# A two-layer transformer kernel on one core: the modulation weights in column quarters, each followed by a quarter of the first projection

## The chip, the cores and the metric

One core of a Trainium2 chip runs the whole program. The metric is the device time of one execution in microseconds (us), as the median of several. TensorE multiplies into eight accumulation banks; ScalarE (ACT), VectorE (DVE) and GpSimd (POOL) prepare operands and read results; SyncE (SP) only issues DMA transfers. The engines run side by side and meet at semaphores.

## The reference

The program is a hybrid attention layer followed by a second layer with a recurrent mixer, latent attention and a large feed-forward part. All data are float32, one batch of 256 tokens, width 2048. The change touches the start of the first layer only:

```
mod = silu(c) @ w_ada + b_ada                      # c: 2048, w_ada: 2048 x 6144
shift, scale, gate = split(mod, 3)
h = rms_norm(x, g_norm) * (1 + scale) + shift      # x: 256 x 2048
proj = h @ w_in                                    # 2048 x 9296
qa, ka, va, za, q_idx, k_idx, w_idx, qb, kb, vb, zb = split(proj)
k_idx = rms_norm(k_idx)
score = sum over 16 index heads of w_idx * relu(q_idx . k_idx)   # per query and key
# the 64 best keys of each query (top_k of score) are kept in attention a
```

`h` at feature f needs `scale` and `shift` at f alone, but a sum over f in `h @ w_in` needs every feature of `h` in the end. The third part of `mod`, the gate, is used after attention and stays where it was.

## The kernel before

**Operands.** A float32 product is made of three single-pass products: each operand is split into a high and a low part (high times high, high times low, low times high). Activations of 256 tokens lie in `HX`, with the halves `HH` and `HL`, as 16 groups of 128 features. A weight chunk of 512 columns comes in four pieces of 512 rows (1 MB each) through the ring `WR` of `NSLOT` = 4 slots. For each piece ACT writes the high part to `WH` in two halves (the helper `high`, L1400), POOL subtracts to get the low part `WL`, in two halves as well (`low_part`, L541), and PE multiplies (L838 to L840). `WH` holds two pieces, so `high` runs two pieces ahead of PE: it waits for `half_done` and `piece_done`. SP waits for a slot to come free and issues the next load (L577). PE's order is the order of the program's text, piece by piece.

**The start.** `w_ada`'s first 4096 columns are needed for shift and scale. They come as 32 pieces of 1 MB, each 128 rows by 2048 contiguous columns (`ada_row`, L590): 16 for scale, then 16 for shift, through the same ring `WR`. For each, `ada_piece` (L895) makes four matmuls with 32 columns of `CW` (the vector c, 32 times over) into the four partition groups of `BANK[0]` or `BANK[1]`. Between the eighth and the ninth piece PE transposes the parameters (L945) and x (L916). After the sixteenth piece ACT copies the bank to `mod_row`, and `mod_cols` (L903) turns the row into columns; after the thirty-second again. DVE adds the bias (L1788). Then ACT scales and shifts the 16 feature groups of x (L1465), and DVE splits each pair of groups in two instructions (L1799, L1800); `ht_ready` tells PE.

**The index part.** Then come a piece for the index key and the index weights (`n_kw`, 128 columns), and two chunks for the index queries (`n_qi`), with features on partitions (`feat_chunk`, stationary operand the weights, 256 moving columns). The index key is normalised by DVE, turned by PE and copied by ACT to `KB`. Sixteen scoring steps follow (L981): PE multiplies queries with `KB` into `BANK[4]` or `BANK[5]`, ACT takes relu of it (L1491), DVE adds it to the score with two instructions (L1825, L1827). Then DVE alone finds the 64 best keys and builds `bias_a` (L1833 to L1859).

**The branch chunks.** Sixteen chunks follow, eight for branch a (queries 0 and 1, keys 2 and 3, values 4 and 5, gates 6 and 7) and eight for branch b, in a hardware loop over b (`Fori`) on PE, DVE and SP. They have tokens on partitions (`tok_chunk`, 512 moving columns, alternating between the bank pairs 0,1 and 2,3). ACT reads each finished chunk (`read_chunk`, L1413). For the first four of a branch DVE normalises the heads (L1868 to L1875), PE transposes them (L996) into `BANK[4]` to `BANK[7]`, and ACT stores them (L1522). Attention follows, and the rest of the program.

## Time and profile before

| | us |
|---|---|
| median of 3 runs | 2029.04 (2020.97 to 2036.34) |
| profiled execution | 2021.87 |
| its span in the profile | 2020.0 |
| PE busy | 1902.7 (94%) |
| POOL busy | 1327.0 (66%) |
| DVE busy | 911.4 (45%) |
| ACT busy | 810.3 (40%) |

The first two rows are of different executions; the profiled one is 7 us below the median. The span is what the trace covers. "Busy" counts the instructions of an engine that do work; PE's is a sum over overlapping, pipelined matmuls, so that 94% doesn't say that it runs at its best speed.

### The profile page before, as it was taken

To read this page: it belongs to the slowest core of one execution; us is meant where nothing else is said; L and a number is where in the kernel's file an instruction comes from. 1 tells how busy PE (TensorE), PEld (TensorE's weight loads), DVE (VectorE), ACT (ScalarE), POOL (GpSimd) and SP (SyncE) were. 2 spreads that over 40 slices of the span, in tenths; PEclk is the share of its full clock that TensorE was granted. 3 is DMA by queue.
4 is the path that set the end of the run, shared out by engine and by line. 5 is a ranking of instruction groups with operands and counts; after the bars stand their busy time and mean duration, and the time that the engine had idled before them with its cause. 6 is when DMAs were issued, how large, how long until landed. Compare 5 with 4: busy or idle time off the path is not lost.

```text
span 2020.0 us, 32437 instructions
## 1 busy us (share of the span) xinstructions
PE 1902.7 (94%) x13007; PEld 1586.7 (79%) x13007; DVE 911.4 (45%) x1117; ACT 810.3 (40%) x1087; POOL 1327.0 (66%) x671
## 2 busy tenths in 40 slices
PE   5679999999999989998999999899999999999997
PEld 2177788788757779887779978788888888888886
DVE  0035760053063251664754350477655566833323
ACT  2044444444453445333422244444443344443333
POOL 0065888888616858994243279598888888844442
PEclk9689999999999999998999999999999999999999
DMA  8943555555593536553200045455555555555553
GB/s 335 411 154 115 178 187 188 188 185 187 202 344 125 179 114 198 189 190 110 76 24 4 4 150 198 151 189 187 187 188 188 190 189 193 192 190 188 198 196 125
DMA packets 161587, 352.64 MB, mean 175 GB/s; under 512 B 6175, under 2 KB 18861, under 8 KB 154829
## 3 DMA queue, kind: packets, MB, share of 16 engines
q1 hardware_dynamic: 160589, 346.94, 51.1%
q10 hardware_dynamic: 896, 4.20, 0.5%
q8 instruction: 81, 1.33, 0.3%
q14 instruction: 21, 0.17, 0.0%
HBM read 349.02 MB, written 2.10 MB: 174 GB/s over the span
## 4 chain that ended last, share of the span: by engine, by line
PE 59%; POOL 19%; issue 14%; DMA 4%; DVE 2%; ACT 1%; POOLq 0%; DVEq 0%; SPq 0%; ACTq 0%
PE bank L884 20%; POOL WL L541 19%; PE bank L886 10%; PE bank L838 6%; PE bank L840 6%; PE bank L839 6%; PE bank L1185 5%; DMA WR<-in_w_ada 3%; PE bank L1105 1%; PE bank L1115 1%; PE bank L895 1%; PE bank L916 1%; PE bank L1148 0%; DMA WR<-in_w_in 0%; PE bank L917 0%
## 5 line engine op out<-in xcount | busy, mean ns | idle before, releaser
L541 POOL TENSOR_TENSOR WL<-WR,WH 128x1024 fp32r<-128x1024 f32 (+2 forms) x510 | 1232.5, 2429 | 512.5 <-ACT WH L1400 511.3
L1400 ACT ACTIVATE WH<-WR 128x1024 fp32r<-128x1024 f32 (+2 forms) x554 | 576.9, 1047 | 809.6 <-PE bank L840 462.2
L884 PE MATMUL bank<-HX,WH 128*128 128x512 f32 x1840 | 640.3, 392 | 6.5 <-POOL WL L541 5.3
L886 PE MATMUL bank<-HX,WL 128*128 128x256 f32 x1840 | 515.2, 280 | 0.0
L884 PEld LDWEIGHTS bank<-HX,WH 128*128 128x128 f32 x1840 | 344.2, 187 | 83.1 <-issue 6.0
L886 PEld LDWEIGHTS bank<-HX,WL 128*128 128x128 f32 x1840 | 347.7, 189 | 0.0
L838 PE MATMUL bank<-WH,HX 128*128 128x512 f32 (+2 forms) x864 | 335.2, 388 | 12.5 <-POOL WL L541 6.3
L839 PE MATMUL bank<-WL,HX 128*128 128x512 f32 (+2 forms) x864 | 332.5, 385 | 0.0
L840 PE MATMUL bank<-WH,HX 128*128 128x512 f32 (+2 forms) x864 | 332.3, 385 | 0.0
L838 PEld LDWEIGHTS bank<-WH,HX 128*128 128x128 f32 x864 | 163.7, 189 | 45.9 <-issue 11.4
L840 PEld LDWEIGHTS bank<-WH,HX 128*128 128x128 f32 x864 | 163.6, 189 | 30.6
L839 PEld LDWEIGHTS bank<-WL,HX 128*128 128x128 f32 x864 | 163.8, 190 | 30.0 <-issue 0.2
L1951 DVE TENSOR_REDUCE arena<-bank 128x256 f32<-128x512 f32 x115 | 71.3, 681 | 207.7 <-PE bank L886 207.7
L840 PE MATMUL bank<-WH,AL 128*128 128x512 f32 x352 | 137.0, 389 | 0.0
L839 PE MATMUL bank<-WL,AH 128*128 128x512 f32 x352 | 136.9, 389 | 0.0
L838 PE MATMUL bank<-WH,AH 128*128 128x512 f32 x352 | 136.9, 389 | 0.0
L541 DVE TENSOR_TENSOR WL<-WR,WH 128x1024 fp32r<-128x1024 f32 x44 | 53.9, 1226 | 157.9 <-ACT WH L1400 157.8
L895 PE MATMUL bank<-WR,CW 128*32 128x512 f32 x384 | 69.9, 815 | 31.5 <-DMA WR<-in_w_ada 31.5
L2184 DVE SCALAR_TENSOR_TENSOR arena<-arena,cols 128x256 f32<-128x256 f32 x44 | 90.0, 2103 | 1.6 <-DVE arena L2179 1.5
L1875 DVE TENSOR_SCALAR arena<-arena,small 128x128 f32<-128x128 f32 x64 | 61.5, 1030 | 43.1 <-ACT small L1408 43.1
L2189 DVE SCALAR_TENSOR_TENSOR arena<-arena,cols 128x256 f32<-128x256 f32 x44 | 78.8, 1848 | 1.5
L840 PEld LDWEIGHTS bank<-WH,AL 128*128 128x128 f32 x352 | 66.1, 188 | 13.8
(288 smaller groups left out, 1957.6 us busy)
## 6 DMA issues: line engine op xcount, KB each, us to landing
WR<-in_w_in SPq DMA_DIRECT2D x97, 1024.0 KB, 5.0
WR<-in_w_ada SPq DMA_DIRECT2D x48, 1024.0 KB, 7.9
WR<-in_ffn_w_gate SPq DMA_DIRECT2D x44, 1024.0 KB, 5.1
WR<-in_ffn_w_up SPq DMA_DIRECT2D x44, 1024.0 KB, 5.2
WR<-in_ffn_w_down SPq DMA_DIRECT2D x44, 1024.0 KB, 5.0
WR<-in_w_out SPq DMA_DIRECT2D x32, 1024.0 KB, 5.0
WR<-in_w_in SPq DMA_DIRECT2D x12, 768.0 KB, 4.3
WR<-in_mla_w_ukv SPq DMA_DIRECT2D x4, 1024.0 KB, 5.6
```

Source lines behind the costliest of these rows:

```text
L541: eng.tensor_tensor(half(WL, n % NSLOT, *w), half(WR, n % NSLOT, *w), half(WH, nth(n) % 2, *w), ALU.subtract).then_inc(ready, 1)
L838: pe.matmul(out, stat[0], mov[0], start=start, stop=False, skip_group_check=True)
L839: pe.matmul(out, stat[0], mov[1], start=False, stop=False, skip_group_check=True)
L840: return pe.matmul(out, stat[1], mov[0], start=False, stop=stop, skip_group_check=True)
L884: pe.matmul(bank[:, :].rearrange("p (h n) -> p h n", h=2), wh[:, k, o], HX[:, :, kk, :], start=kk == 0, stop=False, skip_group_check=True)
L886: last = pe.matmul(bank[:, 0:L], wl[:, k, o], HX[:, 0, kk, :], start=False, stop=kk == KT - 1, skip_group_check=True)
L895: last = pe.matmul(bank[o, :], CW[:, k, :], WR[:, n % NSLOT, g * CH:(g + 1) * CH], start=k == 0, stop=k == KT - 1)
L1185: last = pe.matmul(o[h, q, :], x(h, q), y(h, q), start=(n == 0), stop=(n == len(terms) - 1))
L1400: act.activation(half(WH, nth(n) % 2, *w), half(WR, n % NSLOT, *w), ACT.Copy).then_inc(hi_ready, 1)
L1951: dve.tensor_reduce(dst, BANK[bank][:, :].rearrange("p (h n) -> p n h", h=2), AX_X, ALU.add).then_inc(ready, 1)
L2184: own.mark(dve.scalar_tensor_tensor(out=CV[:, f, :], in0=RAWF[:, f, 1:L + 1], scalar=w(1), in1=CV[:, f, :], op0=ALU.mult, op1=ALU.add))
L2189: last = dve.scalar_tensor_tensor(out=CV[:, f, :], in0=RAWF[:, f, 0:L], scalar=w(0), in1=CV[:, f, :], op0=ALU.mult, op1=ALU.add)
```

## The change

**Loads.** The 4096 columns of `w_ada` are taken in four column quarters: quarter m holds 512 columns of shift and the same 512 of scale, for all 2048 rows, as 8 pieces of 1 MB (256 rows by 2 times 512 columns), each in two transfers whose contiguous stretch is 512 columns (2 KB). They have a ring of their own in the arena (`ada_w`, four slots of 1 MB, semaphores `ada_in` and `ada_done`). Between them SP loads `w_in`: for each quarter q of the rows, one piece for the index key (128 columns), two for the index queries and one for the first chunk of branch a (`in_piece`).

**Work.** After quarter q of `w_ada`, `mod_cols(q)` gives shift and scale of 4 of the 16 feature groups, which ACT scales and DVE splits. PE then multiplies the rows of quarter q of all four pieces into banks that stay open over the four quarters: `BANK[1]` key, `BANK[4]` to `BANK[7]` queries, `BANK[2]` and `BANK[3]` branch chunk; `BANK[0]` holds the modulation. Between these pieces stand the 8 `mod_piece` of quarter q+1.

**Scores.** The sixteen scoring steps move from before the first branch chunk into chunks 5 and 6 of branch a, one before every second feature group on PE, and one relu before each `high` on ACT. DVE chooses the keys after the fourth chunk of branch a. The loop over b is written out on PE and DVE, and SP's is split in two. The slot numbers of later pieces shift; of the last output projection's loads the third no longer waits for `y_sum`, the fourth does.

The diff, cut to its core:

```diff
-        mod_row = at(4096, 2, CH)
+        mod_row = at(4096, CH)
+        CA = at(4608, KT, 32)
+        ada_w = [at(8192 + PK * CH * i, PK * CH) for i in range(4)]
...
+            w_mod = w_ada[:, 0:2 * D].rearrange("(i k p) (h c n) -> i c p k h n", k=2, p=P, h=2, c=4)
+
+            def ada_quarter(m, first, end):
+
+                for i in range(first, end):
+                    n = 8 * m + i
+                    if n >= 4:
+                        sp.wait_ge(ada_done, n - 3)
+                    for k in range(2):
+                        sp.dma_start(ada_w[n % 4][:, k * 2 * CH:(k + 1) * 2 * CH].rearrange("p (h n) -> p h n", h=2),
+                                     w_mod[i, m, :, k]).then_inc(ada_in[n % 4], 16)
+
+            def in_piece(q, i):
+
+                c0, width = ((KW_COL, P), (IDX_COL, CH), (IDX_COL + CH, CH), (0, CH))[i]
+                src = w_in[q * PK * P:(q + 1) * PK * P, c0:c0 + width]
+                load(n_in + 4 * q + i, src.rearrange("(k p) n -> p k n", p=P), width)
+
+            ada_quarter(0, 0, 4)
...
+            ada_quarter(0, 4, 8)
+            for q in range(4):
+                in_piece(q, 0)
+                in_piece(q, 1)
+                if q < 3:
+                    ada_quarter(q + 1, 0, 3)
+                in_piece(q, 2)
+                if q < 3:
+                    ada_quarter(q + 1, 3, 5)
+                in_piece(q, 3)
+                if q < 3:
+                    ada_quarter(q + 1, 5, 8)
+            with sp.Fori(1, 8) as j:
+                chunk(n_br, w_in, j * CH, CH, shift=j * PIECES)
+            with sp.Fori(0, 8) as j:
+                chunk(n_br + 8 * PIECES, w_in, B_COL + j * CH, CH, shift=j * PIECES)
...
-                elif m == 2:
+                elif m == 3:
...
+            def mod_piece(n):
+
+                i = n % 8
+                pe.wait_ge(ada_in[n % 4], 32 * (n // 4 + 1))
+                if i == 0 and n >= 8:
+                    pe.wait_ge(mod_ready, n // 8)
+                for g in range(4):
+                    o = slice(32 * g, 32 * g + 32)
+                    last = pe.matmul(BANK[0][o, :], CA[:, 2 * i + g // 2, :], ada_w[n % 4][:, g * CH:(g + 1) * CH],
+                                     start=i == 0, stop=i == 7)
+                last.then_inc(ada_done, 1)
+
             def mod_cols(m):
 
                 pe.wait_ge(row_took, m + 1)
                 for j in range(4):
-                    last = pe.matmul(BANK[2 + m][:, 4 * j:4 * j + 4], mod_row[:, m, j * P:(j + 1) * P], group_col,
+                    last = pe.matmul(BANK[0][:, 2 * j:2 * j + 2], mod_row[:, j * P:(j + 1) * P], half_col,
                                      start=True, stop=True)
                 last.then_inc(mod_cols_ready, 1)
...
-            for k in range(KT // 2):
-                ada_piece(n_ada + k, k, BANK[0])
+            for n in range(4):
+                mod_piece(n)
...
-            for k in range(KT // 2, KT):
-                ada_piece(n_ada + k, k, BANK[0])
-            for k in range(KT):
-                ada_piece(n_ada + KT + k, k, BANK[1])
-                if k == 3:
-                    mod_cols(0)
-            mod_cols(1)
...
+            for n in range(4, 8):
+                mod_piece(n)
+            for q in range(4):
+                more = 8 * (q + 1)
+                mod_cols(q)
+                for i, (token, first, width) in enumerate(((False, 1, P), (False, 4, CH), (False, 6, CH), (True, 2, CH))):
+                    if q < 3:
+                        for n in range(*((0, 3), (3, 5), (5, 7), (7, 8))[i]):
+                            mod_piece(more + n)
+                    piece(n_in + 4 * q + i, q, token, first, width)
+                    if q == 3 and i == 1:
+                        pe.wait_ge(kiT_taken, 1)
+                        for t in range(TT):
+                            last = pe.transpose(BANK[0][:, t * P:t * P + P], KIT[:, t * P:(t + 1) * P], ident[:])
+                        last.then_inc(ki_ready, 1)
...
+            def index_from(s):
+
+                def begin(kk):
+                    if kk % 2 == 1:
+                        index_step(s + kk // 2)
+                return begin
+
+            for b in range(2):
                 for j in range(8):
 
+                    if b == 0 and j == 0:
+                        continue
+                    if b == 0 and j == 1:
+                        pe.wait_ge(kb_ready, 1)
                     pe.wait_ge(act_took, b * 16 + 6 + 2 * j - 2)
-                    tok_chunk(n_br + PIECES * j, (j + 1) % 2, CH, more=b * (8 * PIECES))
+                    tok_chunk(n_br + PIECES * j, (j + 1) % 2, CH, more=b * (8 * PIECES),
+                              **(dict(begin=index_from(8 * (j - 5))) if b == 0 and j in (5, 6) else {}))
...
+            for q in range(4):
+                act.wait_ge(ada_done, 8 * (q + 1))
+                act.activation(mod_row, BANK[0][:, :], ACT.Copy).then_inc(row_took, 1)
+                high(n_in + 4 * q)
+                act.wait_ge(mod_ready, q + 1)
+                for k in range(4 * q, 4 * q + 4):
+                    act.activation(xT[:, k, :], xT[:, k, :], ACT.Identity, bias=mod[:, k:k + 1],
+                                   scale=gs[:, k:k + 1]).then_inc(x_scaled, 1)
+                high(n_in + 4 * q + 1)
+                if q == 3:
+                    act.wait_ge(piece_done, n_in + 13)
+                    act.activation(KIT, BANK[1][:, 0:L], ACT.Copy).then_inc(kiT_taken, 1)
+                high(n_in + 4 * q + 2)
+                high(n_in + 4 * q + 3)
...
+                    scoring = b == 0 and j in (5, 6)
+                    relus = lambda p: dict(first=lambda s: index_relu(8 * (j - 5) + 2 * p + s)) if scoring else {}
+                    if b or j:
+                        high(n + 2, more, **relus(0))
+                        high(n + 3, more, **relus(1))
...
+            two_rows = lambda v: v.rearrange("p (h k) -> p h k", h=2)
+            for q in range(4):
+                o = slice(4 * q, 4 * q + 4)
+                dve.wait_ge(mod_cols_ready, q + 1)
+                own.link(dve.tensor_tensor(two_rows(mod[:, 0:2 * KT])[:, :, o],
+                                           BANK[0][:, 0:8].rearrange("p (j h) -> p h j", h=2),
+                                           two_rows(col("b_ada", 0, 2 * KT))[:, :, o], ALU.add))
+                dve.scalar_tensor_tensor(out=gs[:, o], in0=mod[:, KT + 4 * q:KT + 4 * q + 4], scalar=1.0,
+                                         in1=col("g_norm", 4 * q, 4), op0=ALU.add, op1=ALU.mult).then_inc(mod_ready, 1)
+                for g in (2 * q, 2 * q + 1):
+                    k = slice(2 * g, 2 * g + 2)
+                    dve.wait_ge(x_scaled, 2 * (g + 1))
+                    own.link(dve.tensor_copy(HH[:, k, :], xT[:, k, :]))
+                    dve.tensor_tensor(HL[:, k, :], xT[:, k, :], HH[:, k, :], ALU.subtract).then_inc(ht_ready, 1)
...
-            with dve.Fori(0, 2) as b:
-                own.enter(b, 12)
+            for b in range(2):
...
-                own.leave(2)
+                if b == 0:
+                    choose_keys()```

On PE, at the end of the modulation, before: the last two of the 32 pieces, `mod_cols` (L903), and the first products with the index key's weights.

```order
L895 MATMUL bank<-WR,CW 32x512 [waits piece_in2]
L895 MATMUL bank<-WR,CW 32x512 x3
L895 MATMUL bank<-WR,CW 32x512 [waits piece_in3]
L895 MATMUL bank<-WR,CW 32x512 x3
L903 MATMUL bank<-ident,arena 128x4 [waits row_took]
L903 MATMUL bank<-ident,arena 128x4 x3
```

And now, at the end of the first of four quarters: L934 is a modulation piece, L942 `mod_cols`, L865 to L867 the products with the key's piece.

```order
L934 MATMUL bank<-arena 32x512 [waits ada_in3]
L934 MATMUL bank<-arena 32x512 x3
L942 MATMUL bank<-small,arena 128x2 [waits row_took]
L942 MATMUL bank<-small,arena 128x2 x3
L934 MATMUL bank<-arena 32x512 [waits mod_ready,ada_in0]
L934 MATMUL bank<-arena 32x512 x3
L934 MATMUL bank<-arena 32x512 [waits ada_in1]
L934 MATMUL bank<-arena 32x512 x3
L934 MATMUL bank<-arena 32x512 [waits ada_in2]
L934 MATMUL bank<-arena 32x512 x3
L865 MATMUL bank<-HX,WH 128x256 [waits lo_ready,ht_ready]
L866 MATMUL bank<-HX,WH 128x256
```

Products now stand after 8 modulation pieces and `mod_cols`, with three pieces of the next quarter ahead of them; before they stood after all 32.

On SP, the loads after the parameters, before (L590 is `w_ada`, L577 `w_in`):

```order
L590 DMA WR<-in_w_ada 128x2048 [waits piece_done] x28
L577 DMA WR<-in_w_in 128x16x128 [waits piece_done]
L577 DMA WR<-in_w_in 128x4x512 [waits piece_done] x8
```

And now, in the first quarter (L605 is `w_ada`, L581 `w_in`):

```order
L581 DMA WR<-in_w_in 128x4x128
L581 DMA WR<-in_w_in 128x4x512
L605 DMA arena<-in_w_ada 128x2x512 [waits ada_done]
L605 DMA arena<-in_w_ada 128x2x512
L605 DMA arena<-in_w_ada 128x2x512 [waits ada_done]
L605 DMA arena<-in_w_ada 128x2x512
L605 DMA arena<-in_w_ada 128x2x512 [waits ada_done]
L605 DMA arena<-in_w_ada 128x2x512
L581 DMA WR<-in_w_in 128x4x512
```

Loads of both matrices alternate in one queue, each kind with waits for its own ring.

On ACT, the scoring steps before: the last of sixteen relus (L1491), and behind them the `high` of the first branch chunk (L1400).

```order
L1491 ACTIVATE arena<-bank 128x256 [waits relu_used,idx_ready]
L1491 ACTIVATE arena<-bank 128x512 [waits relu_used,idx_ready]
L1491 ACTIVATE arena<-bank 128x256 [waits relu_used,idx_ready]
L1491 ACTIVATE arena<-bank 128x512 [waits relu_used,idx_ready]
L1400 ACTIVATE WH<-WR 128x1024 [waits half_done,piece_in3]
L1400 ACTIVATE WH<-WR 128x1024 [waits piece_done]
```

And now, in chunk 5 of branch a (L1572 is relu, L1474 `high`):

```order
L1572 ACTIVATE arena<-bank 128x256 [waits idx_ready]
L1474 ACTIVATE WH<-WR 128x1024 [waits half_done,piece_in2]
L1572 ACTIVATE arena<-bank 128x512 [waits idx_ready]
L1474 ACTIVATE WH<-WR 128x1024 [waits piece_done]
L1572 ACTIVATE arena<-bank 128x256 [waits relu_used,idx_ready]
L1474 ACTIVATE WH<-WR 128x1024 [waits half_done,piece_in3]
L1572 ACTIVATE arena<-bank 128x512 [waits relu_used,idx_ready]
L1474 ACTIVATE WH<-WR 128x1024 [waits piece_done]
```

A relu now stands ahead of each half of the high part, and each waits for PE's scoring matmul and, through `relu_used`, for DVE.

## Rows read from the trace of the kernel before

**Rows 1.** Waits of PE, 0 to 620 us: in total, times, longest.

```profile
PE bank L895 <- DMA WR<-in_w_ada: 31.5, 28, 3.9
PE bank L838 <- DVE HX L1800: 11.4, 3, 7.9
...
PE bank L996 <- DVE arena L1875: 2.7, 1, 2.7
...
PE bank L838 <- ACT arena L1413: 1.9, 1, 1.9
```

**Rows 2.** Windows: length, busy us (instructions) per engine, PE clock, DMA share, GB/s.

```profile
25.00:50.00 25.00, 20.88 (x140) 10.46 (x132) 1.08 (x8) 4.78 (x8) 0.00 (x0) 1.00 0.79 320
50.00:75.00 25.00, 18.76 (x84) 3.51 (x80) 0.54 (x3) 0.60 (x1) 0.00 (x0) 0.57 1.01 423
44.00:92.00 48.00, 32.41 (x172) 5.50 (x164) 0.54 (x3) 0.60 (x1) 0.00 (x0) 0.70 0.99 406
101.00:104.00 3.00, 1.53 (x8) 1.44 (x7) 0.18 (x1) 2.00 (x2) 1.39 (x1) 0.50 1.06 391
125.00:150.00 25.00, 25.00 (x211) 25.00 (x210) 2.46 (x2) 10.38 (x13) 20.84 (x9) 1.00 0.59 200
312.00:334.00 22.00, 22.00 (x99) 18.22 (x98) 0.00 (x0) 9.46 (x10) 19.41 (x9) 1.00 0.58 192
```

**Rows 3.** Timeline of PE, 0 to 60 us.

```profile
31.83 1.94 PE L895 MATMUL bank<-WR,CW 128*32 128x512 f32 x8 [0.55 <-DMA WR<-in_w_ada]
...
34.72 8.42 PE L916 MATMUL bank<-diag,X 128*128 128x128 f32 x64
43.07 3.64 PE L895 MATMUL bank<-WR,CW 128*32 128x512 f32 x32
```

**Rows 4.** Timeline of DVE, 0 to 170 us: `diag` for the transposes of x.

```profile
21.53 0.48 DVE L1758 TENSOR_SCALAR diag<-ident,small 128x128 f32<-128x128 f32 x2 [1.15 <-ACT small L1408]
```

**Rows 5.** Timeline of all engines, 88 to 128 us.

```profile
98.01 1.94 PE L895 MATMUL bank<-WR,CW 128*32 128x512 f32 x8 [0.75 <-DMA WR<-in_w_ada]
...
106.09 7.96 ACT L1465 ACTIVATE arena<-arena,small 128x256 f32<-128x256 f32 x16
107.20 0.43 DVE L1799 CAST HX<-arena 128x512 fp32r<-128x512 f32 x1 [4.38 <-ACT arena L1465]
107.66 2.71 DVE L1800 TENSOR_TENSOR HX<-arena,HX 128x512 fp32r<-128x512 f32 x1
...
110.43 0.58 PE L838 MATMUL bank<-HX,WH 128*128 128x256 f32 x1 [7.90 <-DVE HX L1800]
...
118.08 0.28 PE L840 MATMUL bank<-HX,WL 128*128 128x256 f32 x1
```

**Rows 6.** Timeline of ACT, 160 to 400 us: where it reads a finished chunk.

```profile
210.71 1.06 ACT L1413 ACTIVATE arena<-bank 128x512 f32<-128x512 f32 x2
...
232.47 1.06 ACT L1413 ACTIVATE arena<-bank 128x512 f32<-128x512 f32 x2
...
259.64 1.06 ACT L1413 ACTIVATE arena<-bank 128x512 f32<-128x512 f32 x2
...
282.29 1.07 ACT L1413 ACTIVATE arena<-bank 128x512 f32<-128x512 f32 x2
```

**Rows 7.** Timeline of PE, 172 to 190 us: the scoring matmuls.

```profile
171.98 5.08 PE L981 MATMUL bank<-arena 128*128 128x256 f32 x10 [2.17 <-ACT arena L1484]
...
184.98 1.56 PE L981 MATMUL bank<-arena 128*128 128x512 f32 x4 [0.26 <-ACT arena L1491]
```

**Rows 8.** Timeline of DVE, 168 to 260 us: scoring and choice of keys.

```profile
179.60 10.09 DVE L1827 SCALAR_TENSOR_TENSOR arena<-arena 128x256 f32<-128x256 f32 x22 [0.45 <-DVE arena L1827]
...
203.24 2.31 DVE L1855 SCALAR_TENSOR_TENSOR arena<-arena,small 128x128 f32<-128x128 f32 x1
...
224.34 0.43 DVE L1859 TENSOR_TENSOR masks<-masks 128x256 f32<-128x256 f32 x1
```

**Rows 9.** Timeline of POOL, 0 to 240 us.

```profile
191.90 2.41 POOL L541 TENSOR_TENSOR WL<-WR,WH 128x1024 fp32r<-128x1024 f32 x1 [19.00 <-ACT WH L1400]
```

246 lines of the change are left out of this document (112 added, 134 removed).

## Prediction

> **What bounds the kernel now.** I read the waits of PE first. Up to 620 us they are led by 31.5 us for `w_ada` in 28 waits, then 11.4 us in 3 waits for DVE's split of x at the first product [rows 1]. So the start is bound by transfers, and nearly nothing else there is done. The windows say the same: between 44 and 92 us the DMA engines are busy 0.99 of the time at 406 GB/s, POOL does nothing, and PE's busy time is only that of the modulation matmuls, at a mean clock of 0.70 [rows 2]. From 125 us on it is the other way: PE busy 25.00 of 25.00 us, DMA share 0.59 [rows 2]. Two stages that need different things stand one behind the other.
>
> The timeline gives the stations. The last `w_ada` matmuls start at 98.01, ACT scales x from 106.09 (16 instructions in 7.96 us), DVE splits, and the first product starts at 110.43 [rows 5]. The scoring matmuls begin at 171.98 [rows 7], POOL idles for 19.00 us while they run [rows 9], and ACT reads the first branch chunk at 210.71 [rows 6]. So the change can gain in 0 to 210.71 us, the point at which `BANK[2]` and `BANK[3]` hold branch chunk 0 and chunk 1 begins.
>
> **Part 1: `w_ada` in quarters with products between.** The price of one quarter is the larger of its transfers and its PE work.
>
> Transfers: 8 pieces of `w_ada` (8.39 MB), three `w_in` pieces of 1.05 MB and the key's quarter of 0.26 MB, 11.8 MB. `w_ada` now comes in stretches of 2 KB where it came in 8 KB. The windows show both kinds with the queue full: 423 GB/s for `w_ada` at 8 KB, 391 GB/s at 101 to 104 us, when `w_in` at 2 KB is moved [rows 2]. I take 391, since that queue is as full as the new one will be: 11.8 MB / 391 GB/s = 30.2 us. The bounds are 27.9 us (423 GB/s) and 35 us, if I scale the unfilled queue (200 GB/s at share 0.59, thus 339; 192 at 0.58, thus 331 [rows 2]).
>
> PE: the moving operands give 25.00 us / 211 = 0.118 us per 256-column product, and 22.00 / 99 = 0.222 us per 512-column one [rows 2]. The key's quarter has 4 x 3 = 12 of the first (1.4 us), each query piece 4 x 4 x 3 = 48 (5.7 us, twice), the branch piece 4 x 2 x 3 = 24 of the second (5.3 us): 18.1 us. The modulation pieces take 3.64 us / 4 = 0.9 us each with data there [rows 3]; with 1.0 us, eight are 8.0 us, and `mod_cols` with its waits about 1. Sum 27.1 us at full clock. So a quarter in the steady state lasts 30.2 us and is bound by transfers, by a little.
>
> Does PE's fixed order spoil that? SP may be four `w_ada` pieces and three to four `w_in` pieces ahead, each over 2.7 us of transfer. The order rows put 3, 2, 2 and 1 modulation pieces before the four products. Following the two rings through a quarter by hand, each load finds its slot free before the queue reaches it, unless PE is over 4 us late. The first quarter is worse: nothing has been loaded ahead.
>
> The start: the eighth piece arrives at 31.83 now, and the transposes of x take 8.42 us after it [rows 3]. In the new order the transposes stand after the fourth piece. They need `diag`, ready at 21.53 + 0.48 = 22 us [rows 4], and ACT's copies between them, so they are over by 31; the eighth piece arrives 8 percent later, near 34, and is multiplied by 35. ACT's copy, `mod_cols`, the bias and two scales at 7.96 / 16 = 0.5 us each [rows 5] bring the first product to about 40 to 45; it then waits for pieces 9 and 10 of the next quarter, which arrive behind two `w_in` pieces. By the queue (2.7 us per MB), the branch piece of quarter 0 ends at 74, and at 79 with the clock's price below. Quarters 1 and 2 end at 107 and 136. A second count checks this: all transfers up to the last `w_ada` piece are 33.6 + 3 x 3.4 + 3 (x and parameters) = 46.8 MB, 120 us at 391 GB/s, with the start and the gap at the parameters 125 us; behind it stand 1 modulation piece and two products, 12 us: 137.
>
> The last quarter has no transfers to wait for. Exposed: `mod_cols`, bias, two scales, a split (0.43 + 0.69 us at best; L1800 took 2.71 us beside POOL [rows 5]), 4 us; then 18.1 us of products, of which the second is held by `high` and POOL for 1 to 2 us, since ACT writes it only behind the scales: 24 us, thus 160. The index key is turned after the second product, so that ACT's and DVE's work on it lies beside the last two (11 us); its square root stands behind `high` in ACT's queue until the third product ends, and DVE's four small instructions then run beside POOL. Turning and copying `KB`: 2 to 3 us in the open. Chunk 1 starts at 163, for 210.71 now [rows 6]: **-47.7 us**. Bounds: 154 (423 GB/s) and 183 (335 GB/s: 46.8 MB last 140 us).
>
> **The clock.** While PE waits for `w_ada` its clock falls: 0.57 from 50 to 75 us, though 1.00 in 25 to 50 us, when it had 140 matmuls and 20.88 us of work [rows 2]. The products from 110.43 ran at half clock and were at full clock by 118.08, after unbroken work [rows 5]. I charge this once, 3.7 us, in the first quarter, and not later, since PE then has 27 us of work in 30. The Trainium skill ("TensorE: Matmul & The Clock Gate", HAM oscillation) has a rule against this: where each tile's compute is shorter than the wait for its data, every tile starts at the low clock. By it the quarters would be priced at the low clock, as in rival 1; this trace agrees for the bare `w_ada` pieces (0.57), and shows no mixture of both.
>
> **Part 2: the scoring in chunks 5 and 6.** Its PE work moves and isn't hidden, since PE bounds the chunks: 8 pairs of 1.56 us [rows 7] are **+12.5 us**. ACT's relu waits for the scoring matmul, and `high`, then POOL's low part, then PE are queued behind it. But PE's next half piece is 12 products of 0.222 us = 2.7 us, and the relu takes less. DVE: two instructions per step took 10.09 / 22 = 0.46 us each with POOL idle [rows 8]; beside POOL one took 2.31 us [rows 8]. A step lasts 2.7 + 0.78 = 3.5 us, of which POOL works 2.41 [rows 9]; in the remaining 1.1 us two short ones fit, and one that is held still leaves the pair under 3.5. I take nothing; the bounds are 0 and +20 us (rival 3). The choice of keys lasts from 179.60 + 10.09 = 189.7 to 224.8 us now [rows 8], 35 us; it then starts at the end of chunk 6 and has chunk 7 and two chunks of branch b, 65 us, before PE wants a head from DVE: hidden.
>
> **Part 3: what the scoring held up.** Now DVE still chooses keys when chunk 1 ends. Chunk 2 takes 259.64 - 232.47 = 27.2 us, for 282.29 - 259.64 = 22.65 of chunk 3 [rows 6]; PE's own wait is 2.7 of that [rows 1]. With DVE free: **-4.5 us** (bounds -4.5 and -2.7).
>
> **Part 4: the written-out loop.** The wait of 1.9 us on L838 [rows 1] stands at the loop's turn, behind nothing in the order: **-1.9 us** (bounds -1.9 and, if more code costs as much, +1.9). The freed wait of the third load of the last projection: nothing, since `high` comes later than that load today.
>
> **Sum.** -47.7 + 12.5 - 4.5 - 1.9 = -41.6. The profiled execution took 2021.87, so 1980.3; it is 7.2 us under the median of 2029.04, and on that median the forecast is **1987**.
>
> **Rivals.** 1. *The low clock rules the quarters (slower).* PE stops for each load, never gets the full clock, and its work per quarter is 2 x 27.1 = 54 us instead of 30: +72 for three, 2059. It needs the mean clock to stay low; from 44 us per quarter (30.2 + 41.6 / 3), a mean clock of 27.1 / 44 = 0.62, the change loses. For it: 0.57 and 0.70 today [rows 2]. Against: products are unbroken work of over 5 us, and at half clock PE would be the bound and no longer wait, which brings the clock back, as after 110.43.
>
> 2. *Transfers are worse than the full queue suggests.* At 335 GB/s, or with stops at the rings, 183 instead of 163: +20, 2007. For: the other `w_in` rows give 331 to 339, in half-filled queues. Against: the 391 row.
>
> 3. *The scores pace chunks 5 and 6.* If DVE pays 2.35 us for each of 32 instructions, 75 us stand against 16 x 3.5 = 56: +20, 2007. Against: a late relu delays POOL too, and then DVE is fast.
>
> 4. *No real overlap.* If PE's order and the rings make transfers and products take turns, a quarter is 30.2 + 18.1 = 48 us, +54, 2041: the change wouldn't do what it says.
>
> **Chances.** Forecast 0.70, rival 1 0.05, rival 2 0.15, rival 3 0.07, rival 4 0.03. The measurement of this kernel can't tell less than about 1 percent, 20 us, from nothing: the bound is 2009. Of rivals 2 and 3, two thirds lie under it. Faster 0.70 + 0.15 = 0.85, same 0.07, slower 0.08. Range: from 1972 (27.9 us per quarter, chunk 1 at 154, and 6 us for the spread of the runs) to 2012 (rivals 2 or 3, and 5 us).
>
> **What would show it.** In the profile after: `w_ada` matmuls and products alternating from about 40 us; DMA share near 1 until about 125 us with 380 to 395 GB/s; PE clock over 0.9 in quarters 1 and 2; `ht_ready` waits of some 4 us only once; the first branch chunk read by ACT near 160; chunks 5 and 6 each 6 us longer than chunk 3, with DVE's score instructions under 3.5 us per pair; no wait of the head transposes of chunk 1 for DVE. Wrong would be: GB/s near 335, clock near 0.6, or chunks 5 and 6 over 32 us.

## The result, and the profile after

| | before | after |
|---|---|---|
| median, same chip | 2030.52 (2020.97 to 2036.34) | 1997.74 (1996.98 to 2002.26) |
| profiled execution | 2021.87 | 1997.8 |
| its span | 2020.0 | 1996.1 |

The ratio is 0.9854 with a 95% interval of 0.9825 to 0.9883: faster by 1.5%, some 30 us, clear of the interval. The median of 1997.74 lies inside the range of the forecast (1972 to 2012), on the forecast side, and 11 us above the forecast of 1987.

**The waits.** PE's waits from 0 to 620 us after the change (total, times, longest) answer to [rows 1].

```profile
PE bank L934 <- DMA arena<-in_w_ada: 22.5, 12, 8.6
PE bank L865 <- DVE HX L1851: 4.3, 1, 4.3
...
PE bank L865 <- POOL WL L545: 3.3, 3, 1.5
PE bank L865 <- DVE HX L1884: 2.8, 1, 2.8
...
PE bank L1030 <- DVE arena L1895: 1.1, 1, 1.1
...
PE bank L865 <- ACT arena L1563: 0.7, 1, 0.7
```

PE still waits 22.5 us for `w_ada` (31.5 before), but in 12 waits instead of 28. Of the 11.4 us for DVE's split (then L1800, now L1884) 2.8 are left, in the last quarter; the 2.7 us of the head transposes and the 1.9 us at the loop's turn are gone.

**The quarters.** The windows after the change answer to [rows 2]: length, busy us (instructions) of PE, PEld, DVE, ACT and POOL, PE clock, DMA share, GB/s.

```profile
25.00:50.00 25.00, 20.22 (x134) 12.05 (x133) 3.87 (x14) 9.95 (x17) 6.16 (x4) 0.82 1.04 377
50.00:75.00 25.00, 22.50 (x151) 16.97 (x151) 0.00 (x0) 5.28 (x7) 9.60 (x5) 0.84 1.00 361
75.00:100.00 25.00, 21.85 (x151) 14.82 (x150) 2.48 (x6) 8.09 (x11) 14.57 (x8) 0.93 1.01 359
100.00:125.00 25.00, 22.68 (x165) 16.86 (x165) 2.48 (x6) 7.57 (x12) 11.19 (x7) 1.00 1.03 374
125.00:150.00 25.00, 21.06 (x138) 16.60 (x137) 2.48 (x6) 8.03 (x13) 9.99 (x7) 0.94 0.61 210
146.00:152.00 6.00, 5.27 (x24) 4.73 (x25) 1.04 (x3) 3.98 (x5) 5.17 (x3) 0.56 0.44 139
152.00:158.00 6.00, 6.00 (x46) 6.00 (x46) 0.00 (x0) 1.75 (x2) 6.00 (x3) 0.87 0.22 87
```

Transfers and products do lie beside each other: from 25 to 125 us the DMA share is 1.00 to 1.04 and PE is busy 20 to 23 us of 25. But the full queue moves only 359 to 377 GB/s. The clock, 0.57 from 50 to 75 us before [rows 2], is now 0.82 to 1.00 in these windows. From 146 us, where PE no longer waits for transfers, it is 0.56 again.

**The last quarter.** PE's timeline shows why.

```profile
142.35 0.95 PE L942 MATMUL bank<-small,arena 128*128 128x2 f32 x8
146.06 0.39 PE L865 MATMUL bank<-HX,WH 128*128 128x256 f32 x1 [2.77 <-DVE HX L1884]
...
168.32 0.39 PE L867 MATMUL bank<-WH,HX 128*128 128x512 f32 x1
169.83 0.63 PE L1030 MATMUL bank<-ident,arena 128*128 128x128 f32 x4 [1.12 <-DVE arena L1895]
171.15 0.50 PE L865 MATMUL bank<-WH,HX 128*128 128x512 f32 x1 [0.69 <-ACT arena L1563]
```

The first line is `mod_cols(3)`. From its start to the first product are 3.7 us, and the half clock stands right behind them. The last product starts at 168.32; 2.4 us after its end, with the turned key between, chunk 1 starts at 171.15. The four `mod_cols` start at 38.13, 79.31, 111.65 and 142.35, so quarter 0 (from one `mod_cols` to the next) takes 41.2 us, quarter 1 32.3 and quarter 2 30.7.

**The chunks.** ACT's reads of finished chunks answer to [rows 6]: chunks 0 to 4, 5, 6 (behind a table load) and 7.

```profile
170.99 1.08 ACT L1487 ACTIVATE arena<-bank 128x512 f32<-128x512 f32 x2
194.20 1.07 ACT L1487 ACTIVATE arena<-bank 128x512 f32<-128x512 f32 x2
216.87 1.07 ACT L1487 ACTIVATE arena<-bank 128x512 f32<-128x512 f32 x2
239.54 1.07 ACT L1487 ACTIVATE arena<-bank 128x512 f32<-128x512 f32 x2
262.20 1.07 ACT L1487 ACTIVATE arena<-bank 128x512 f32<-128x512 f32 x2
290.32 1.07 ACT L1487 ACTIVATE arena<-bank 128x512 f32<-128x512 f32 x2
...
318.98 1.09 ACT L1487 ACTIVATE arena<-bank 128x512 f32<-128x512 f32 x2
339.36 1.06 ACT L1487 ACTIVATE arena<-bank 128x512 f32<-128x512 f32 x2
```

Chunk 0 is read at 170.99 for 210.71 before: -39.7 us. Chunk 1 takes 23.2 us for 21.8: +1.4. Chunk 2 takes 22.67 for 27.17: -4.5. From the read of chunk 4 to that of chunk 7 pass 77.16 us; the kernel before with the loop written out (below) needs 66.19: +11.0, the scoring. The first chunk of branch b, 24.0 us before, takes 21.76: -2.2. The sum is -34.0, and attention's first matmul indeed starts at 517.3 for 551.3 before.

**The end.** The kernel after is 34.0 us ahead at attention, but only 23.9 us at the end of the span. The difference is lost where the change has edited nothing. ScalarE's silu over the feed-forward part, before and then after (minimum/median/maximum ns, first and last start):

```profile
L1723 ACT ACTIVATE arena<-arena x11: 1043/1062/1065, 1329.8 to 1769.7; 128x1024 f32<-128x1024 f32 x11
```

```profile
L1808 ACT ACTIVATE arena<-arena x11: 1042/1043/1063, 1297.0 to 1745.8; 128x1024 f32<-128x1024 f32 x11
```

The lead is 32.8 us at the first silu and 23.9 at the last: the same loop takes 448.8 us instead of 439.9, at a granted clock of 1.00 in both. Whether that is the change's doing was the first question for the experiments.

### The profile page after: what moved, and what is told of

Same layout as the page of the kernel before. It is cut to its first block, busy times and chain, and to the rows that moved or that the text cites. A ratio compares the mean times of both kernels' runs of the same rounds, so it can differ in the third digit from the quotient of the medians.

```text
span 1996.1 us, 32360 instructions
## 1 busy us (share of the span) xinstructions
PE 1900.8 (95%) x13023; PEld 1590.4 (80%) x13023; DVE 893.0 (45%) x1122; ACT 810.7 (41%) x1095; POOL 1322.8 (66%) x677
## 4 chain that ended last, share of the span: by engine, by line
PE 59%; POOL 20%; issue 18%; DVE 2%; ACT 1%; POOLq 0%; DVEq 0%; ACTq 0%
PE bank L911 21%; POOL WL L545 19%; PE bank L913 10%; PE bank L865 6%; PE bank L866 6%; PE bank L867 6%; PE bank L1257 5%; PE bank L1177 1%; PE bank L1187 1%; PE bank L1220 1%; PE bank L393 0%; POOLq L544 0%; DVE arena L2192 0%; POOL arena L812 0%; PE bank L1364 0%
## 5 line engine op out<-in xcount | busy, mean ns | idle before, releaser
L545 POOL TENSOR_TENSOR WL<-WR,WH 128x1024 fp32r<-128x1024 f32 (+2 forms) x516 | 1227.8, 2390 | 495.2 <-ACT WH L1474 493.9
L1474 ACT ACTIVATE WH<-WR 128x1024 fp32r<-128x1024 f32 (+2 forms) x560 | 577.3, 1037 | 815.6 <-PE bank L867 451.8
L911 PE MATMUL bank<-HX,WH 128*128 128x512 f32 x1840 | 651.8, 399 | 6.9 <-POOL WL L545 5.3
L865 PE MATMUL bank<-WH,HX 128*128 128x512 f32 (+2 forms) x864 | 340.2, 394 | 11.3 <-POOL WL L545 6.3
L866 PE MATMUL bank<-WL,HX 128*128 128x512 f32 (+2 forms) x864 | 332.5, 385 | 0.0
L867 PE MATMUL bank<-WH,HX 128*128 128x512 f32 (+2 forms) x864 | 332.5, 385 | 0.0
L865 PEld LDWEIGHTS bank<-WH,HX 128*128 128x128 f32 x864 | 163.7, 189 | 48.1 <-issue 13.3
L866 PEld LDWEIGHTS bank<-WL,HX 128*128 128x128 f32 x864 | 163.9, 190 | 31.3 <-issue 1.9
L867 PEld LDWEIGHTS bank<-WH,HX 128*128 128x128 f32 x864 | 163.7, 190 | 31.2
L865 PE MATMUL bank<-WH,AH 128*128 128x512 f32 x352 | 136.9, 389 | 0.0
L866 PE MATMUL bank<-WL,AH 128*128 128x512 f32 x352 | 136.9, 389 | 0.0
L867 PE MATMUL bank<-WH,AL 128*128 128x512 f32 x352 | 136.9, 389 | 0.0
L545 DVE TENSOR_TENSOR WL<-WR,WH 128x1024 fp32r<-128x1024 f32 x44 | 53.9, 1226 | 159.0 <-ACT WH L1474 159.0
L1960 DVE TENSOR_SCALAR arena<-arena,small 128x128 f32<-128x128 f32 x64 | 63.7, 1065 | 47.8 <-ACT small L1482 47.8
L2275 DVE SCALAR_TENSOR_TENSOR arena<-arena,cols 128x256 f32<-128x256 f32 x44 | 83.3, 1950 | 1.5
L865 PEld LDWEIGHTS bank<-WH,AH 128*128 128x128 f32 x352 | 66.1, 188 | 13.8
L867 PEld LDWEIGHTS bank<-WH,AL 128*128 128x128 f32 x352 | 66.1, 188 | 13.7
L866 PEld LDWEIGHTS bank<-WL,AH 128*128 128x128 f32 x352 | 66.1, 188 | 13.5
```

The lines of the kernel that those rows point to most:

```text
L545: eng.tensor_tensor(half(WL, n % NSLOT, *w), half(WR, n % NSLOT, *w), half(WH, nth(n) % 2, *w), ALU.subtract).then_inc(ready, 1)
L865: pe.matmul(out, stat[0], mov[0], start=start, stop=False, skip_group_check=True)
L866: pe.matmul(out, stat[0], mov[1], start=False, stop=False, skip_group_check=True)
L867: return pe.matmul(out, stat[1], mov[0], start=False, stop=stop, skip_group_check=True)
L911: pe.matmul(bank[:, :].rearrange("p (h n) -> p h n", h=2), wh[:, k, o], HX[:, :, kk, :], start=kk == 0, stop=False, skip_group_check=True)
L1474: act.activation(half(WH, nth(n) % 2, *w), half(WR, n % NSLOT, *w), ACT.Copy).then_inc(hi_ready, 1)
```

## The experiments

The end time carries things that differ between executions of one kernel, as will be seen. So each run is read at stations of its profile: `mod_cols(3)`, ACT's reads, attention's first matmul, first and last silu. The end times and ratios stand beside them.

### The kernel before, once more

No edit.

> The kernel before, unchanged, profiled a second time. The profile after is 34.0 us ahead of the one before when attention starts (516.09 for 550.08) but only 23.9 us at the end; 9 us are given back in the feed-forward loop, whose first wide matmul lasts 398 ns in the median instead of 391. Theory A: that pace differs from execution to execution, so this run may show 391 or 398 ns, and its span lies anywhere from 2020 to 2035 us. Theory B: it is a property of the changed program (its later pieces lie in other slots), so this run shows 391 ns and about 2020 us again.

Measured: 2031.34 us (2020.53 to 2034.49, 10 runs), span 2030.5. Attention starts at 552.0 (551.3 in the first profile), silu runs from 1331.4 to 1780.2, that is 448.8 us. One line of each profile shows the wide product of the feed-forward part from 1400 to 1700 us, ns minimum/median/maximum; first the earlier profile of this kernel, then this one:

```profile
L884 PE MATMUL bank<-HX,WH x867: 391/391/392, 1399.7 to 1699.9; 128*128 128x512 f32 x174
```

```profile
L884 PE MATMUL bank<-HX,WH x850: 394/398/404, 1399.9 to 1699.9; 128*128 128x512 f32 x170
```

It is the same program, and 867 instructions in one execution stand against 850 in the other. So the pace belongs to the execution and not to the change. The first profile of the kernel before had the quick pace, the first one after the slow one; of the difference between their end times 9 us are this.

### The kernel after, once more

No edit.

> The changed kernel again, unchanged. Theory A: 9 us of the missing gain are the feed-forward loop's pace, which an execution has or has not (391 or 398 ns from one 512-column matmul to the next), so its runs here fall into two groups near 1988 and 1997 or all near one of them, while the start of attention stays within 3 us of 517.3. Theory B: the pace belongs to the changed program: all runs at 1995 to 2002, and the feed-forward loop takes 448 us again.

Measured: 1990.98 us (1986.87, 1987.97, 1993.99, 1997.30), ratio 0.9835 [0.9812, 0.9859]. The profiled execution has a span of 1995.6, `mod_cols(3)` at 142.65, the read of chunk 0 at 170.36 and attention at 516.7, close to the first profile (142.35, 170.99, 517.3). The feed-forward loop has the quick pace this time:

```profile
L1808 ACT ACTIVATE arena<-arena x11: 1043/1062/1065, 1305.4 to 1745.3; 128x1024 f32<-128x1024 f32 x11
```

439.9 us, so theory A holds. Yet the end is no earlier, since the first silu comes at 1305.4 instead of 1297.0. The windows from 980 to 1020 us show a second such place: first this execution, then the first one of the same kernel.

```profile
980.00:1020.00 40.00, 37.61 (x355) 26.84 (x357) 12.93 (x28) 9.29 (x21) 15.98 (x33) 0.66 0.16 54
```

```profile
980.00:1020.00 40.00, 37.07 (x617) 28.90 (x617) 18.95 (x45) 11.98 (x30) 17.93 (x38) 0.96 0.17 55
```

PE gets 355 matmuls done at a mean clock of 0.66, and 617 at 0.96. So there are two places, each worth some 9 us, in which executions of one kernel differ. Of the twelve profiled executions of this document four have the slow pace in the feed-forward loop (448.8 us), and this one alone has the low clock at 980 to 1020 us. An execution of the kernel after that is spared both would end near 1987, by my estimate (1996.1 - 8.9).

### The loop over b written out, alone

The kernel before, with this edit on PE and the like on DVE:

```diff
-            with pe.Fori(0, 2) as b:
+            for b in range(2):
```

> The kernel before with only the loop over the two branches written out on PE and DVE. If the 1.9 us wait is the loop's turn, attention starts 2 us earlier (548) and the wait on the first product of branch b is gone. If it is a real wait for a chunk's read, nothing moves. Feed-forward pace: theory A either value, theory B 391 ns.

Measured: 2026.67 us, ratio 0.9994 [0.997, 1.0018], attention at 545.4. The first chunk of branch b takes 21.76 us instead of 23.96 (23.83 in the second profile of the kernel before): -2.2, as foreseen. The rest of the lead at attention, 3.7 us against the first profile, is not the edit's: this execution is 2 to 3 us ahead already at 168 us, before anything that the edit touches. The start varies by that much, and the ratio can't show 2 us.

### Late scores, without the quarters

The kernel of the last run, with the scoring taken from before chunk 1 into chunks 5 and 6, and the choice of keys behind chunk 4's head work:

```diff
-            for s in range(16):
-                index_step(s)
...
+                    tok_chunk(n_br + PIECES * j, (j + 1) % 2, CH, more=b * (8 * PIECES),
+                              **(dict(begin=index_from(8 * (j - 5))) if b == 0 and j in (5, 6) else {}))
...
```

> The kernel before with the loop written out and the scoring steps in chunks 5 and 6 and the choice of keys behind branch a's head work, but w_ada whole and first as before. Theory: the scoring stage (17.5 us between the last query product and chunk 0) and the 4.5 us of chunk 2 go, 11 us come back in chunks 5 and 6, 2 us from the loop: attention starts 13 us earlier than before, at 537 us, 14 us before the 2 us of the loop are taken off being wrong by no more than 2. Rival: the stage's time was needed by DVE anyway and shows up later, so that only 2 to 4 us are won and the quarters make the rest.

Measured: 2020.87 us, ratio 0.9951 [0.9927, 0.9976], attention at 539.3. Against the run before: the scoring stage gives back 12.8 us, chunk 2 gives 4.15, chunks 5 and 6 cost 10.95. The net -6.0 is less than the 11 expected without the loop, since the scoring stage cost 12.8 us where it stood and not 17.5.

### Quarters, with early scores

The kernel after, with the reverse of that edit:

```diff
+            pe.wait_ge(kb_ready, 1)
+            pe.wait_ge(act_took, 6)
+            for s in range(16):
+                index_step(s)
...
```

> The changed kernel with the scoring steps back before chunk 1 and the choice of keys before the head work. Theory: 17 us for the stage and 4.5 us for chunk 2 come back, 11 us in chunks 5 and 6 go: attention starts 10 to 11 us later than in the changed kernel, at 527 us. The quarters alone are then worth 21 us against before. Rival: as above, no more than 4 us later. Feed-forward pace: theory A either, theory B 398 ns.

Measured: 2010.16 us, ratio 0.9919 [0.9891, 0.9947], attention at 530.5, 13.2 us later than with late scores (expected: 10 to 11). Together with the two runs above, the 34.0 us divide so: loop 2.2; quarters alone 14.9 (530.5 against 545.4), for which I had expected 21; late scores on top 13.2; and 3.7 are spread over runs. Late scores alone were worth 6.0. So the two parts help each other, by 7.2 us. Only 1.9 of them lie before the read of chunk 0 (14.7 us for 12.8); 3.7 lie in chunk 1 and 1.6 in chunk 2. PE's waits show what stands there:

```profile
PE bank L1070 <- DVE arena L1967: 7.9, 1, 7.9
```

These are the head transposes, which wait for DVE, and DVE is behind with the choice of keys: it ends it at 205.7 us and has only then time for the heads. In the run with the loop alone the same wait is 2.5 us. There chunks 0 and 1 both follow the scoring steps and cover DVE's work; with quarters chunk 0 is done before them, and chunk 1 alone must cover it. PE then does nothing from 208 to 214 us, and its clock is 0.50 from 214 to 218. With late scores both go.

### Longer stretches

The kernel after, with each modulation piece fetched as whole rows of 2048 columns, in one transfer instead of two. Bytes, order and matmuls stay, but the modulation is made from other columns of `w_ada`, so the kernel no longer computes the reference's output. The core of the edit:

```diff
-                    for k in range(2):
-                        sp.dma_start(ada_w[n % 4][:, k * 2 * CH:(k + 1) * 2 * CH].rearrange("p (h n) -> p h n", h=2),
-                                     w_mod[i, m, :, k]).then_inc(ada_in[n % 4], 16)
+                    r = n % 16
+                    sp.dma_start(ada_w[n % 4], w_ada[r * P:(r + 1) * P, (n // 16) * D:(n // 16 + 1) * D]).then_inc(ada_in[n % 4], 16)
...
```

> The changed kernel with each modulation piece fetched as one transfer of 128 stretches of 8 KB (a whole row's 2048 columns) in place of 512 stretches of 2 KB in two transfers; bytes, order and matmuls are the same, but the modulation is computed from other columns of w_ada, so the output is another. Theory A, the transfers' rate (367 to 377 GB/s with the share of the queues at 1.02 to 1.05) is what makes the quarters 30 to 41 us long: at the 423 GB/s of the kernel before's 8 KB rows the quarters shorten by 10 to 12%, mod_cols(3) comes near 135 instead of 142.35, chunk 1 near 164 instead of 171.15, attention near 510 instead of 517.3. Theory B, TensorE with its low clock and the ring of four buffers bounds them: mod_cols(3) stays within 1.5 us of 142.35 and attention within 2 us of 517.3.

Measured: 1985.04 us, ratio 0.9774 [0.9746, 0.9803]. `mod_cols(3)` 136.2 (I had expected near 135), read of chunk 0 164.78, attention 511.1: 6.2 us ahead, of 7 expected. The windows, first of the kernel after (with quarter 2 as well), then of this run:

```profile
38.00:80.00 42.00, 35.31 (x211) 23.80 (x212) 2.79 (x6) 10.00 (x16) 17.02 (x10) 0.80 1.02 369
80.00:112.00 32.00, 28.85 (x203) 20.64 (x203) 2.48 (x6) 9.23 (x13) 15.63 (x8) 0.95 1.02 367
112.00:142.00 30.00, 27.17 (x201) 19.55 (x201) 2.48 (x6) 9.23 (x13) 15.69 (x8) 1.00 0.84 296
```

```profile
38.00:80.00 42.00, 36.51 (x242) 23.84 (x242) 5.26 (x12) 13.21 (x20) 17.62 (x11) 0.88 1.00 396
80.00:112.00 32.00, 29.59 (x219) 20.89 (x217) 2.48 (x6) 11.37 (x16) 18.11 (x10) 1.00 1.01 398
```

The longer stretch, with half as many transfers, is worth 27 to 31 GB/s while the share stays at 1: the rate sets these quarters, and theory A is right. Which of the two, the stretch or the number of transfers, gives the rate is not separated here.

### Half the modulation's transfers

The kernel after; from the fifth modulation piece on the second of the two transfers isn't made. Half of each piece keeps old contents, so this kernel too computes something else; PE's work is unchanged.

```diff
-                    for k in range(2):
+                    for k in range(2 if n < 4 else 1):
...
```

> The changed kernel, but from the fifth modulation piece on only the first of the two transfers of each piece is made (the other half of the buffer keeps old contents, so the modulation is another). TensorE's work is unchanged, the modulation's transfers are half. Theory A (transfers bound the first three quarters): what is left is TensorE's own 27 us per quarter at full clock, mod_cols(3) comes at 120 to 125 instead of 142.35 and attention at 497 to 500 instead of 517.3. Theory B (TensorE's own work at a clock of 0.8 to 0.95 fills the quarters already): quarters stay at 30 us or more, mod_cols(3) not before 135, attention not before 510.

Measured: 1978.15 us, ratio 0.977 [0.973, 0.9811]; `mod_cols` at 38.8, 70.5, about 98.5 and 126.5, attention at 501.2, both a little later than I had expected for theory A (120 to 125, and 497 to 500).

```profile
38.00:80.00 42.00, 38.48 (x283) 25.76 (x280) 5.26 (x12) 16.41 (x24) 22.16 (x13) 0.96 0.84 292
80.00:112.00 32.00, 31.45 (x239) 24.33 (x237) 2.47 (x6) 10.30 (x14) 19.68 (x10) 1.00 0.82 284
```

The quarters last 31.7, 28 and 28 us instead of 41.2, 32.3 and 30.7, PE is busy 31.45 of 32.00 us, and the clock is 0.96 to 1.00. This is the floor that PE's own work sets, 28 us (my estimate was 27.1). It also shows that the clock in the quarters follows from the waits: with most of them gone it is 0.96 and 1.00, for 0.80 and 0.95. In the last quarter, whose wait for DVE's split is still there, it falls as before (0.54 from 130 to 136 us).

### The index key turned later

The kernel after, with the turning inside chunk 1 at its ninth step, `KB`'s copy behind ACT's first reads for chunk 1, and, in all four quarters, ACT's `high` for the first piece of the index queries ahead of its wait for the modulation. The PE part of the first of these:

```diff
-            pe.wait_ge(act_took, 4)
-            pe.wait_ge(kix_ready, 4)
-            for lo in range(2):
+            def turn_key(kk):
+
+                if kk == 8:
+                    pe.wait_ge(act_took, 4)
+                    pe.wait_ge(kix_ready, 4)
+                    for lo in range(2):
...
```

> The changed kernel with the turning of the index key moved from between the last quarter and chunk 1 into chunk 1 (at its ninth step), its copy on ScalarE put behind the first reads for chunk 1, and ScalarE's scaling for the low parts issued without a wait for the modulation of the quarter. Theory A: the 2.0 to 2.6 us between the last product of the quarters (168.32) and chunk 1's first (171.15) go, and nothing else changes: chunk 1 near 168.8, attention near 514.5 instead of 517.3. Theory B: the gap only covered something that is late anyway (HX of the first steps of chunk 1, or the first weights): chunk 1 starts early but waits, attention stays within 1 us of 517.3.

Measured: 1986.19 us (1984.92 to 1994.77), ratio 0.9805 [0.9769, 0.984], read of chunk 0 at 167.99, chunk 1 22.3 us instead of 23.2, attention at 513.4: -3.9 us. But this execution's `mod_cols(3)` is 1.5 us early (140.8). That may be the execution, or ACT's earlier `high`, which acts in every quarter: the three quarters take 102.0 us here and 102.5 in the last run below, which has this edit too, but 103.6 to 104.8 in the four executions without it and with all transfers as they were. Behind `mod_cols(3)` the edit is worth 1.5 to 2.4 us (372.6 us to attention, for 374.1 and 375.0 in the two executions of the kernel after), of about 3 expected. The run doesn't separate its two parts. PE's waits from 142 to 200 us are a single one, 3.8 us for the split. So the gap in front of chunk 1 covered nothing that was late anyway, and of the 1.4 us by which chunk 1 had become longer 0.9 belong to it. The clock still falls, to 0.55 from 146 to 152 us.

### PE kept busy in the pause

The kernel after, with matmuls whose result nobody reads:

```diff
+                    if q == 3 and i == 0:
+                        pe.wait_ge(mod_ready, 4)
+                        for _ in range(6):
+                            pe.matmul(BANK[0][:, 256:512], ident[:], X[:, 0, 0:L], start=True, stop=True)
                     piece(n_in + 4 * q + i, q, token, first, width)
```

> The changed kernel with six full-precision matmuls of 256 columns (about 2.6 us at full clock) on TensorE in front of the last quarter's first product, in the 2.5 us in which TensorE otherwise waits for the scaled rows; nobody reads their result. Theory A: it is this pause of 4 us from 142.35 to 146.06 after which the granted clock drops to 0.56 and 0.87: with TensorE busy in it the clock stays above 0.9 from 146 to 158, the last product comes 2 to 3 us sooner than 168.32 (about 165.5) and attention at 514 to 515.5. Theory B: GpSimd's rows of the last quarter (six of 14.22 us in all without a pause) or DVE's, not the clock, pace it: the clock stays up and the last product still comes at 168.

Measured: 1992.63 us, ratio 0.9821 [0.9792, 0.9849]. The clock is 1.00 from 142 to 170 us. From `mod_cols(3)` to the start of the last product pass 24.1 us (144.1 to 168.23), where the two executions of the kernel after need 26.0 and 25.0. The last product still comes at 168, as theory B said, but only because `mod_cols(3)`, which stands ahead of the edit, is 1.7 us late in this execution. And the gain doesn't last: PE then waits 4.0 us for DVE where it waited 1.1, and chunk 0 is read at 174.00. Behind this wait the clock falls once more; first the kernel after, then this run:

```profile
176.00:182.00 6.00, 6.00 (x28) 4.95 (x28) 0.00 (x0) 2.12 (x2) 5.36 (x3) 1.00 0.52 175
```

```profile
176.00:182.00 6.00, 6.00 (x20) 4.81 (x19) 1.94 (x4) 1.06 (x1) 1.12 (x1) 0.69 0.00 0
```

Chunk 1 takes 25.8 us instead of 23.2, and attention starts at 522.9, 5.6 us later than in the kernel after, where I had expected 514 to 515.5. DVE's timeline says what holds PE; first the kernel after, then this run.

```profile
158.65 2.49 DVE L1888 TENSOR_TENSOR arena<-arena 128x64 f32<-128x64 f32 x1 [11.57 <-ACT arena L1547]
161.17 0.22 DVE L1889 TENSOR_REDUCE small<-arena 128x1 f32<-128x64 f32 x1
161.43 0.22 DVE L1888 TENSOR_TENSOR arena<-arena 128x64 f32<-128x64 f32 x1
...
161.94 2.09 DVE L1828 TENSOR_SCALAR small<-small 128x2 f32<-128x2 f32 x1
...
164.50 5.18 DVE L1895 SCALAR_TENSOR_TENSOR arena<-arena,small 128x64 f32<-128x64 f32 x4 [0.27 <-ACT small L1482]
```

```profile
158.55 2.01 DVE L1892 TENSOR_TENSOR arena<-arena 128x64 f32<-128x64 f32 x1 [9.75 <-ACT arena L1551]
160.59 0.22 DVE L1893 TENSOR_REDUCE small<-arena 128x1 f32<-128x64 f32 x1
160.85 2.07 DVE L1892 TENSOR_TENSOR arena<-arena 128x64 f32<-128x64 f32 x1
```

```profile
148.57 23.80 POOL L545 TENSOR_TENSOR WL<-WR,WH 128x1024 fp32r<-128x1024 f32 x10 [7.53 <-ACT WH L1478]
```

The same 128x64 instruction takes 0.22 us or 2.0 to 2.5, and one of POOL's takes 2.38 (23.80 / 10, the last line, this run's POOL). In this execution of the kernel after POOL pauses 0.3 to 0.6 us between its pieces from 161 us on, waiting for ACT, and the second product of the pair slips through a pause. In this run POOL runs ten in a row without a pause, both products pay, and the four scalings take 6.75 us instead of 5.18. From its first product to its last scaling DVE needs 13.9 us here. It needs 11.0 in both executions of the kernel after, though in the second POOL runs eight in a row and the second product pays 2.07 us too, and 11.3 in the last run below, with TensorE at full clock as well. So how DVE's small instructions fall between POOL's decides; that a full clock always closes POOL's pauses is not shown.

That is what the Trainium skill says in "SBUF — State Buffer", section "SBUF: two separate sides": DVE and GpSimd share one pair of ports as an exclusive lock for a whole instruction, which a DVE instruction with two SBUF inputs needs against a GpSimd one that reads SBUF. The trace agrees for the products (2.0 to 2.5 us beside POOL, 0.22 without) and for the reductions with one input, which take 0.22 all the same. L1828, with one input, pays too (2.09). The page names a performance mode as a second condition; no run here tells whether that is it.

### Both edits

The last two edits together.

> The kernel with the index key turned inside chunk 1 (as in the run before with that edit) and the six extra matmuls in front of the last quarter's first product. Theory A: the extra matmuls did keep the clock, and what made their run late was only DVE, whose small operations on the index key each lasted as long as one operation of GpSimd (2.0 to 2.4 us) and came at 172.6 in front of chunk 1. With nobody before chunk 1 waiting for the key, the clock stays at 1.00 from 142 to 180, the last quarter takes 23.4 us or less from its mod_cols instead of the 24.5 of the run with the key alone, chunk 1 starts 1 to 2 us nearer to mod_cols(3), attention at 511 to 513. Theory B: GpSimd's low parts (2.38 us each, without a pause) pace the quarter as soon as the clock doesn't: attention stays within 0.5 us of 513.4 after subtracting the difference of mod_cols(3).

Measured: 1984.36 us (1979.22 to 1993.87), ratio 0.9822 [0.9785, 0.9858], beside 0.9835 of the kernel after, on the same chip. Read of chunk 0 at 166.88, that is 25.0 us behind `mod_cols(3)` (141.88), for 28.6 and 27.7 in the kernel after and 27.2 with the key alone. Attention starts at 512.3, though `mod_cols(3)` was 1.1 us later than in the run with the key alone. The windows:

```profile
142.00:146.00 4.00, 3.54 (x21) 2.94 (x19) 1.91 (x4) 3.13 (x5) 3.29 (x2) 1.00 0.69 226
146.00:152.00 6.00, 5.42 (x43) 5.08 (x43) 1.61 (x3) 2.62 (x4) 1.88 (x1) 1.00 0.37 120
152.00:158.00 6.00, 6.00 (x53) 6.00 (x52) 2.11 (x3) 3.37 (x7) 6.00 (x4) 1.00 0.58 194
```

43 matmuls from 146 to 152 us instead of 24. Theory A holds: holding the clock is worth 2.2 us, once nobody waits for DVE behind it. To the start of the last product the stretch takes 23.6 us here and 25.8 with the key alone, where I had written 23.4 and 24.5. In the six executions of the quarters with the pause in place it takes 25.0 to 26.4, in the two without 24.1 and 23.6, so the sign is clear and the size less so. By the stations this is the best version that computes the right output, 4.5 to 5 us ahead of the kernel after at attention; by end times (1979 to 1994 against 1987 to 1997) that is likely and not shown.

## Why the prediction was right or wrong

**Right.** The bound at the start (transfers first, then PE) and the direction. Chunk 2: -4.5 forecast and measured (in two other profiles with early scores and the whole `w_ada` first it took 28.5 and 26.8 us where the first had 27.2, so 4.2 to 5.8). The loop's turn: -1.9 forecast, -2.2 measured, and more code cost nothing. The scoring in chunks 5 and 6: +12.5 forecast, +11.0 measured, with DVE's pairs under 1.8 us per step, so that it paces nothing. The choice of keys and `WO2`'s third load: no wait seen. Of the rivals none came in full: the clock was 0.80 to 1.00 in the quarters (rival 1 wanted 0.62 or less), chunks 5 and 6 at 28.1 and 28.7 us (rival 3), the quarters 30.7 to 41.2 us and not 48 (rival 4). Rival 2 came in part: the rate was 367 GB/s, between my 391 and its 335, and some 8 of its 20 us were lost.

**The term that was mis-sized** is part 1, -47.7 forecast, -39.7 measured. Its steps in us:

| step | forecast | measured |
|---|---|---|
| quarter 0 ends | 79 | 79.3 |
| quarter 1 | 28 | 32.3 |
| quarter 2 | 29 | 30.7 |
| last quarter, to the end of its last product | 24 | 26.4 |
| turning of the key | 3 | 2.4 |
| chunk 1 starts | 163 | 171.2 |

"I take 391" was the first fault. The row behind it is 3 us long, at the turn between two kinds of transfer [rows 2]; the full queue with 2 KB stretches moved 359 to 377 GB/s over windows of 25 us. 11.8 MB / 367 = 32.2 us, which is quarter 1 (32.3); in the second execution 375 GB/s would give 31.5, and it takes 31.2. I had even counted quarter 1 at 28, below my own 30.2, and the prediction gives no reason for that. Quarter 2 (30.7 for 29) lies close to PE's floor of 28, with one wait of 1.8 us for a late piece. The run with long rows confirms the rate as the cause (+27 to 31 GB/s, 6.2 us), the one with half the transfers confirms that PE alone would need 28.

Quarter 0 ended where I had it by luck. My 79 was 74 by the queue at 391 GB/s, and 5 on top for the clock. In the run with long rows, at 396 GB/s, it ends at 74.8, although the clock is 0.88 there. I read this so: the clock's price lay beside the transfers and cost next to nothing, and what filled the 5 us was the slower rate. No run holds the clock in quarter 0 to prove it.

The second was "I charge this once, 3.7 us, in the first quarter, and not later". I had listed the exposed chain of the last quarter at 4 us and it was 3.7, but I didn't ask what the clock does behind it: 0.56 and 0.87 for 12 us. The run with both edits prices that at 2.2 us. In the first quarter the clock did fall, to 0.50 from 42 to 50 us, between waits of 1.9, 1.3 and 0.9 us for `w_ada`; in quarters 1 and 2 its mean was 0.95 and 1.00. The Trainium skill's page that I weighed there ("TensorE: Matmul & The Clock Gate", HAM oscillation), by which work begun behind a wait for data starts at the low clock, is borne out in the first quarter, and not as a price of every quarter.

One more was not in the forecast: chunk 1 became 1.4 us longer, 0.9 of it by the turning of the key.

**The sum at attention**: 41.6 forecast, 34.0 measured; 8.0 us from part 1, 1.4 from chunk 1, less 1.5 and 0.3 that scoring and loop did better.

**From attention to the end** I let everything follow unchanged. The mechanism is right (the same instructions), but the profile before was of a quick execution in the feed-forward loop (439.9 us) and the one after of a slow one (448.8). On equal pace 2021.87 - 34.0 is 1988. I lifted the forecast by 7.2 us to the median, and so the forecast of the median that 34.0 would have given is 1995, 3 us from the 1997.7 measured. The kernel after again gave 1987 to 1997.

What stays open: why the wide product runs at 391 ns in some executions and 398 in others, at a clock of 1.00 both times, and what decides the clock at 980 to 1020 us. What set the last 0.5 us of chunk 1 is open too. Nor did I try quarters whose stretches are longer and whose columns are the right ones.
